# The second gate's projections moved beside the first attention, their result in the tiles of the convolution's used inputs

## The reference

```
h = rms_norm(x, norm_mix_g)
q, k, v, c_b, c_c, c_u, g_a, g_b = split(h @ w_in)       # 6 x 512 columns, then 2 x 1024
q, k = rms_norm per head of 64 (8 heads)
branch_a = stick_breaking_attention(q, k, v) @ w_sb_branch
branch_b = (c_b * causal_conv3(c_c * c_u)) @ w_conv_branch
merged = sigmoid(g_a) * branch_a + sigmoid(g_b) * branch_b
x = x + merged @ w_out
```

## Time and profile before

| | before |
|---|---|
| median of 3 runs | 2695.13 us |
| span of the profiled execution | 2693.3 us (the page gives no other time of that execution) |
| TensorE busy | 2439.7 us, 91% |
| VectorE busy | 1723.2 us, 64% |
| ScalarE busy | 1029.1 us, 38% |
| DMA | 605.96 MB, mean 225 GB/s |
| first matmul of the merge | 371.60 us |

### The profile page before, as it was taken

The page is one execution under the profiler, slowest core; times in us unless marked ns, Lnnn a source line. Parts: engine busy times, 40 slices in busy tenths (PEclk is TensorE's granted clock), DMA queues, the critical chain, the costliest instruction groups (busy, mean ns, idle before and its releaser), DMA issues.

```text
span 2693.3 us, 30969 instructions
## 1 busy us (share of the span) xinstructions
PE 2439.7 (91%) x12205; PEld 1864.6 (69%) x12205; DVE 1723.2 (64%) x2984; ACT 1029.1 (38%) x1289; POOL 406.0 (15%) x299
## 2 busy tenths in 40 slices
PE   6888999578777899999989999989999999999996
PEld 4665786333333344677768999989999978777775
DVE  4535344421116657566543998899998578988886
ACT  4744532221004411477232343335655333333333
POOL 0100000000000000000000011132443234454430
PEclk9999999699987999999999999999999999999998
DMA  4454341599990100211022466779999799999992
GB/s 197 169 198 188 125 156 65 192 415 425 425 396 29 63 31 0 94 63 63 32 110 81 157 233 224 255 241 343 343 345 342 278 370 365 382 382 381 380 369 88
DMA packets 159278, 605.96 MB, mean 225 GB/s; under 512 B 13623, under 2 KB 79351, under 8 KB 126488
## 3 DMA queue, kind: packets, MB, share of 16 engines
q1 hardware_dynamic: 91168, 384.32, 37.9%
q0 software_dynamic: 42480, 154.68, 15.4%
q10 hardware_dynamic: 25480, 64.92, 6.2%
HBM read 533.10 MB, written 70.78 MB: 224 GB/s over the span
## 4 chain that ended last, share of the span: by engine, by line
PE 49%; DVE 24%; issue 11%; DMA 9%; ACT 5%; POOL 1%; ACTq 0%; DVEq 0%; SPq 0%; POOLq 0%
DVE window L597 6%; PE P L2590 4%; PE P L2592 4%; PE P L2591 4%; DVE part L597 4%; PE P L2245 3%; PE P L2421 3%; DVE ug L1397 3%; DMA H<-in_w_up 2%; DVE tmp L605 2%; DMA ug<-in_v,sparse 2%; PE P L2041 2%; PE P L2042 2%; PE P L2043 2%; DVE arena L597 1%
## 5 line engine op out<-in xcount | busy, mean ns | idle before, releaser
L597 DVE TENSOR_TENSOR part<-raw,part 128x2048 fp32r<-128x2048 f32 x136 | 311.1, 2288 | 164.2 <-ACT part L1896 162.6
L2590 PE MATMUL P<-hr,part 128*128 128x384 f32 (+1 forms) x1136 | 397.4, 350 | 17.1 <-DVE part L597 16.5
L2592 PE MATMUL P<-hr,part 128*128 128x384 f32 (+1 forms) x1136 | 391.5, 345 | 0.0
L2591 PE MATMUL P<-hr,part 128*128 128x384 f32 (+1 forms) x1136 | 391.3, 344 | 0.0
L2709 POOL DMA_INDIRECT ug<-in_ur,sparse x128 | 179.2, 1400 | 1213.7 <-DVE window L1289 751.2
L2694 PE MATMUL P<-part,ge 128*128 128x512 f32 x768 | 301.9, 393 | 13.3 <-DVE part L597 12.5
L2695 PE MATMUL P<-part,ge 128*128 128x512 f32 x768 | 299.0, 389 | 0.0
L2696 PE MATMUL P<-part,ge 128*128 128x512 f32 x768 | 299.0, 389 | 0.0
L1896 ACT ACTIVATE part<-raw 128x2048 fp32r<-128x2048 f32 x136 | 260.4, 1915 | 99.9 <-PE P L2696 80.8
L2590 PEld LDWEIGHTS P<-hr,part 128*128 128x128 f32 x1136 | 214.6, 189 | 27.9 <-DVE part L597 22.1
L2591 PEld LDWEIGHTS P<-hr,part 128*128 128x128 f32 x1136 | 214.7, 189 | 4.9
(11 more groups left out here) (363 smaller groups left out, 4419.8 us busy)
## 6 DMA issues: line engine op xcount, KB each, us to landing
raw<-in_u SPq DMA_DIRECT2D x64, 1024.0 KB
raw<-in_vd SPq DMA_DIRECT2D x64, 1024.0 KB
W<-in_w_up SPq DMA_DIRECT2D x24, 2048.0 KB, 18.8
W<-in_w_in SPq DMA_DIRECT2D x18, 2048.0 KB, 8.0
W<-in_ada_w SPq DMA_DIRECT2D x12, 2048.0 KB, 7.8
a_scratch<-gt ACTq DMA_DIRECT2D x128, 192.0 KB
w_scratch<-window ACTq DMA_DIRECT2D x12, 2048.0 KB, 11.7
wr<-w_scratch SPq DMA_DIRECT2D x32, 768.0 KB, 13.0
```

The costliest lines, as they stand in the source:

```text
L597: return v.tensor_tensor(out=out_, in0=in0, in1=in1, op=op)
L2590: t.matmul(b, wh[:, k, js], HR[0][:, k, lo:S], start=k == 0, stop=False)
L2591: t.matmul(b, wh[:, k, js], HR[1][:, k, lo:S], start=False, stop=False)
L2592: ins = t.matmul(b, wl[:, k, js], HR[0][:, k, lo:S], start=False, stop=k == 7)
```

## The change

```diff
--- before.py
+++ after.py
@@ -134,13 +134,13 @@
 
         ar = lambda at, n: AR[:, at * S:(at + n) * S].rearrange("p (k n) -> p k n", k=n)
         BH, BL = (ar(8, 4), ar(4, 4)), (ar(12, 4), ar(24, 4))
-        GH, GL = ar(36, 8), ar(28, 8)
+        GH, GL = ar(16, 8), ar(28, 8)
         ONER, LINR = AR[:, 47 * S:47 * S + 128], AR[:, 47 * S + 128:47 * S + 256]
 
 
         B2H, B2L = (ar(0, 4), ar(43, 4)), (ar(14, 4), ar(26, 4))
         G2H, G2L = ar(18, 8), ar(30, 8)
-        HIM = [AR[:, (16 + 4 * i) * S:(20 + 4 * i) * S] for i in range(2)]
+        HIM = [AR[:, (36 + 4 * i) * S:(40 + 4 * i) * S] for i in range(2)]
         parts.close()
         HF = sb("H", 8 * S, f32, early)[:, :]
         H = HF.rearrange("p (k n) -> p k n", k=8)
@@ -177,7 +177,7 @@
 
         Q, K, V, AT = tiles(0, 4), tiles(4, 4), tiles(8, 4), tiles(12, 4)
         CB, CC, CU = tiles(16, 4), tiles(20, 4), tiles(24, 4)
-        GA, GB = tiles(28, 8), tiles(36, 8)
+        GA, GB = tiles(28, 8), tiles(16, 8)
         MOD = MODS[:, 0:96].rearrange("p (k n) -> p k n", n=2)
         G2, GF2 = MODS[:, 112:128], MODS[:, 128:136]
 
@@ -247,20 +247,16 @@
 
 
         beside = []
-        for m in range(5):
-            pj, ada = [("pj", 12 + 4 * m + i) for i in range(4)], [("ada", i) for i in range((0, 3, 6, 9, 11)[m], (3, 6, 9, 11, 12)[m])]
+        for m in range(7):
+            pj, ada = [("pj", 12 + 4 * m + i) for i in range(4)], [("ada", i) for i in range((0, 3, 6, 9, 11, 12, 12)[m], (3, 6, 9, 11, 12, 12, 12)[m])]
             beside += pj[:1] + ada[:1] + pj[1:2] + ada[1:] + pj[2:]
         ORDER1 = []
         for g_ in range(4):
-            for kind, x, n in (("qk", g_, 3), ("sp", 2 * g_, 1), ("tl", 2 * g_, 0), ("sp", 2 * g_ + 1, 1), ("tl", 2 * g_ + 1, 1), ("ex", g_, 1), ("pv", g_, 1)):
+            for kind, x, n in (("qk", g_, 4), ("sp", 2 * g_, 1), ("tl", 2 * g_, 0), ("sp", 2 * g_ + 1, 1), ("tl", 2 * g_ + 1, 1), ("ex", g_, 2 - g_ % 2), ("pv", g_, 1 if g_ < 3 else 0)):
                 ORDER1 += [(kind, x)] + beside[:n]
                 del beside[:n]
-        ORDER1 += beside
-        ORDER1 += [("pj", p) for p in range(32, 40)]
+        ORDER1 += beside[:-2] + [("hp", 0)] + beside[-2:-1] + [("hp", 1)] + beside[-1:] + [("sum", 0), ("ada", 12)]
         ORDER1 += [("mg", n) for n in range(16)]
-
-        ORDER1.insert(max(ORDER1.index(("ada", 11)), ORDER1.index(("pv", 3))) + 2, ("sum", 0))
-        ORDER1.insert(ORDER1.index(("sum", 0)) + 2, ("ada", 12))
 
 
         def att_free(x):
@@ -366,7 +362,8 @@
 
 
 
-        seq_a = [("br", b, c) for b in (1, 0) for c in range(4)] + [("w", 0), ("w", 1)]
+        seq_a = [("br", 0, c) for c in range(4)] + [("w", 0), ("w", 1)] + [("br", 1, c) for c in range(4)]
+        AT_HP = (slice(0, 5), slice(5, 10))
         seq_v = list(seq_a)
         AT_MERGE_A, AT_MERGE_V = {}, {}
         for n in range(16):
@@ -430,7 +427,7 @@
             return key, view(W[i])[:, :, cols], view(HIM[u % 2]), view(WL[i])[:, :, cols]
 
 
-        half_free = lambda u: [("mg_mm", 4 * (u - 2) + 4)] if 2 <= u < 6 else [("op_mm", 2 * (u - 6) + 2)] if u >= 6 else [("cv", 20)]
+        half_free = lambda u: [("mg_mm", 4 * (u - 2) + 4)] if 2 <= u < 6 else [("op_mm", 2 * (u - 6) + 2)] if u >= 6 else [("att_mm", 68)]
         hi_part = lambda u: 9 if u == 0 else 17 + u
         lo_part = lambda u: 15 + u
         n_slot3 = slots.let_go_pj
@@ -736,9 +733,9 @@
                         low_half(i[0] // 2 + 1)
                     if 20 <= i[0] < 24:
                         conv(*i)
-                    if i[0] >= 37:
-                        for x in seq_v[{37: slice(0, 4), 38: slice(4, 8), 39: slice(8, 10)}[i[0]]]:
-                            low_part(x)
+                elif kind == "hp":
+                    for x in seq_v[AT_HP[i[0]]]:
+                        low_part(x)
             dve.wait_ge(s["ada_mm"], 13)
             by_piece = lambda ap: ap.rearrange("p (n c) w -> p n c w", c=4)
             tt(by_piece(MOD), bank[7][:, 0:96].rearrange("p (c n w) -> p n c w", c=4, n=12),
@@ -1546,7 +1543,7 @@
                 act.wait_ge(s["pj_mm"], p + 1)
                 dst = ((Q, K, V, CB, CC)[p // 4] if p < 20 else GA if p < 32 else GB)[:, c if p < 20 else (p - 24) % 8, :]
                 if p >= 32:
-                    act.wait_ge(s["att_mm"], 68)
+                    act.wait_ge(s["cv"], 20)
                 a.activation(dst, b, ACT.Sigmoid if p >= 24 else ACT.Copy).then_inc(s["pj_a"], 1)
 
             for p in range(12):
@@ -1630,9 +1627,9 @@
                         high_half(i[0] // 2 + 1)
                     if not 20 <= i[0] < 24:
                         project(*i)
-                    if 36 <= i[0] < 39:
-                        for x in seq_a[{36: slice(0, 4), 37: slice(4, 8), 38: slice(8, 10)}[i[0]]]:
-                            high_part(x)
+                elif kind == "hp":
+                    for x in seq_a[AT_HP[i[0]]]:
+                        high_part(x)
 
             act.wait_ge(s["att_mm"], 68)
             a.dma_start(WR, A["w_router"].rearrange("(k p) n -> p k n", p=128)).then_inc(s["wr"], 16)
```

## The result

The changed kernel takes 2702.07 us (median of 12 runs) against 2696.3 us before: ratio 1.0020, 95% interval 1.0011 to 1.0028, that is 5.4 us slower (3.0 to 7.6). One of the 12 runs of before took 3496 us; it is left out of the ratio.

A forecast was written before the change was run, and what follows sets the result against it. TensorE's own order was taken to bound the stretch, time changing only through idle and half clock. Idle 23.1 plus half clock 7.2 gave 30.3 against 27.2 us before: +3 us, 2698.1; range -4 to +7.5 us, 2691 to 2702.5.

The forecast's parts named there:

- (1): Tail products 0 and 1: their stalls of 1.6 and 1.1 us go, and nothing is late in their place.
- (2): Tail product 2: its low part is ready in time; the 4.81 us stall and 2.9 of half clock go.
- (6): Weighted sum 2: two projections now stand beside the exponentials; the 2.57 us stall and 1.8 of half clock go.
- (4): Projection 24: new 6.7 us stall for its low half, 2.9 half clock; projection 22's stall (5.34, 2.9) goes.
- (5): Tail product 5 has only an `ada` ahead: stall of 1.1 us; tail product 7's 1.1 goes.
- (7): Projection 30: new 10.5 us stall for its low half behind softplus 3, 2.9 half clock; the earlier 2.99 goes.
- (3): Tail product 3: new 3.5 us stall behind VectorE's convolution and subtractions; 1.4 us taken for uncertain half clock.
- (8): End before the merge: `ada` 12 waits 1.3 us for the modulation-sums copy; merge splits are ready in time.
- (9): New waits and addresses cost nothing, loads just hide, and the 5.39 us stall behind the merge moves along unchanged.
- Rival B: Projections 24 and 30 run wholly at 1.2 GHz behind longer stalls: +10 us, 2705; chance 0.11.
- Rival A: The moved projections fill TensorE's idle places: 20 us won, 2675; chance 0.06.
- C: A load comes late: high half 12's landing at 21 us costs 5 us, 2703; chance 0.03.

The follow-up runs named there:

- the second time: The changed kernel, nothing altered, measured again over five rounds of its own against the kernel before: ratio 1.0014 (1.0005 to 1.0022), 3.8 us slower.
- the first execution: First profiled execution of the changed kernel, nothing altered: merge starts at 374.8 us in place of 371.6; the kernel's first measurement gave ratio 1.0020.
- their own kernel: Kernel before with only the new addresses and waits, its own order kept, measured twice: ratio 1.0007, then 0.9994.
- all four mended: Changed kernel with low halves 12 and 15, high half 12, two convolutions and the modulation-sums copy reordered: 2668.83 us, ratio 0.9892.
- the two other kernels with the same stall: Changed kernel with low half 15 ahead of softplus 3 (ratio 0.9955); changed kernel with idle time ahead of projections 24 and 30 filled by matmuls (0.9993).

## Why the prediction was right, by its own steps

The sign and the places hold, and the stalls to a tenth or two. That the size holds is in part luck. The forecast was +3 us in a range of -4 to +7.5; measured were +5.4 and, the second time, +3.8. But the forecast also had the merge at 373 to 376 us and everything behind moved by the same amount: that is so in the first execution (374.8, +3.2) and not in the other two (370.2 and 370.6), where the stalls and half clock up to the merge explain at most +0.7 of the time.

(1), (2), (6), and the exchanges in (4), (5) and (7): no stall is left ahead of the first three tail products, the third weighted sum, projection 22, projection 28 or tail product 7, by the list of waits. (3) was forecast at 3.5 and measured at 3.34; (4) 6.7 and 6.74; (5) 1.1 and 1.14; (7) 10.5 and 10.37; (8) 1.3 and 1.27. The sum of idle time is 22.9 us against the 23.1 of the forecast. (9) is borne out for the addresses and waits by their own kernel, and for the loads by the list of waits, which holds none. That the causes are those named is shown for (3), (4), (7) and (8) by taking each away ((8) and the whole of (4) only in the kernel with all four mended); for (4) the cause was incomplete, since behind the low half stood the bank of projection 22.

The term that was mis-sized is half clock. I took 2.9 behind each long stall; the first execution has 2.2 behind both (7.96 and 8.03 us in place of 5.8) and the others 1.4 to 1.9. For (3) I took 1.4, the middle of 0 and 2.9: it was 2.9 in one execution and nothing in two, and 1.5 in the two other kernels with the same stall. Behind (8) I took nothing, and two of three have 1.6. The sums are 7.3 us in the first execution, as forecast (7.2) but from other parts, and 4.8 and 5.0 in the others. With 22.9 of idle time that is 30.2 us in the first, +3.0 against the 27.2 of before, and 27.7 and 27.9 in the others, +0.5 and +0.7. A forecast from one execution of before couldn't know that its own clock would repeat and the changed kernel's wouldn't.

Rival B is refuted: projection 30 took 8.03, 7.61 and 7.67 us, less than the 9 from which B was to be told. Behind the stall of 10.4 us half clock cost as much as behind that of 6.7 in the first execution, and 0.4 more in each of the others. By the rule of the Trainium skill (TensorE: Matmul & The Clock Gate, "HAM oscillation") the price is paid at each wait that lets the clock fall; that a longer wait adds nothing was my reading of it. The first execution agrees with that reading (2.2 and 2.2), the others only nearly (1.4 and 1.8, 1.5 and 1.9). Rival A failed for the reason given against it, and C didn't occur.

**What stays open.** The time is 3.8 to 5.4 us over before, while the last matmul of the merge comes only 3.3, 0.3 and 0.7 us later in the three executions. Neither the addresses nor a pure delay of 3.3 us (2.7 measured) account for the rest. From the output projection's first matmul to the end of the span it is 2272.5, 2266.8 and 2276.1 us in the three, and 2267.0 to 2270.3 in five kernels with nearly the same order; in five executions with the order of before it is 2267.6 to 2273.5. The means, 2270.1 and 2269.8, are the same within this scatter, so the profiled executions show no cost of the change behind the merge. They scatter by several us within one kernel: over the two stages from the last matmul of line 2628 to the first of line 2674 (lines of before) the two executions of before take 984.9 and 987.9 us, and the changed kernel's three 989.9, 983.7 and 991.1. There VectorE waits 3.3 to 6.4 us for gathered rows (`ug`) in the executions looked at. The mean of 3.3, 0.3 and 0.7 is 1.4, so some 2 to 4 us of the measured difference have no place in any profile; whether the half clock in the runs that weren't profiled was mostly as dear as in the first one was not settled.

## What to carry to other kernels

When work is moved to cover a wait, what the moved work itself waits for has to be made on the other side of that wait: here the covering projections needed subtractions that stood in VectorE's order behind the very chain they were to cover. So list, for every step put into a gap, the entry that makes each of its inputs and the one that frees its output, on each engine, and ask which stand behind the long chain. Then write the stalls of before and after as a ledger of idle time at places; its sum of idle time was good to 0.3 us here, while the clock behind the stalls, and the stages behind, scattered by as much as the whole effect or more. A single profile of a kernel can't show a difference of that size.

## What the runs showed of the hardware

The granted clock behind the same stall isn't the same in every execution. Behind 3.34 us it was 0.50 once and 1.00 in two others of the same kernel, and a product that takes 2.97 us at full clock took 5.38, 4.43, 4.47 or 2.97; behind 1.27 us, ahead of a step of eight matmuls of 24 columns, it was 1.00 once and 0.72 another time. In the kernel before, stalls of 4.8, 5.3 and 2.6 us had the same price both times, and to 0.2 us in three more executions with its order. And useless matmuls in place of idle time ahead of a step delayed its start by nothing that shows and gave 1.5 and 1.8 us back.
